# Index heads' columns first in the input projection, a split LayerNorm, and tile 1's transposes one weight piece later

## The reference

```
h = x @ w_in[i]
q, k, v, qi, ki, wi, u, vs = split(h)      # 512, 128, 128, 256, 64, 4, 512, 512 columns
rotate part of q, k, qi, ki
score = sum over 4 index heads of relu(qi . ki) * wi ; keep the 64 best keys of each row
a_out = attention over the kept keys
b_out = gelu(u) * (sgu_w (lower triangle) @ LayerNorm(gelu(vs)) + sgu_b)      # the gated half
x = LayerNorm(ALPHA * x + concat(a_out, b_out) @ w_o[i])
x = LayerNorm(ALPHA * x + (silu(gate) * up) @ w_ffn_out + (p[i] @ w_ple[i]) * sigmoid(x @ w_ple_gate[i]))
```

## Time and profile before

| | |
|---|---|
| median of three runs | 1430.33 us (1429.98 to 1430.45) |
| the profiled execution's own time | 1430.49 us |
| its span, first to last instruction | 1428.7 us |
| PE / DVE / ACT / POOL busy | 94% / 66% / 46% / 8% |
| dummy matmuls | 228 |

### The profile page before, as it was taken

The page is one execution under the profiler, slowest core; times in us unless marked ns, Lnnn a source line. Parts: engine busy times, 40 slices in busy tenths (PEclk is TensorE's granted clock), DMA queues, the critical chain, the costliest instruction groups (busy, mean ns, idle before and its releaser), DMA issues.

```text
span 1428.7 us, 16545 instructions
## 1 busy us (share of the span) xinstructions
PE 1342.2 (94%) x6684; PEld 1105.1 (77%) x6684; DVE 941.8 (66%) x1249; ACT 657.2 (46%) x886; POOL 109.8 (8%) x156
## 2 busy tenths in 40 slices
PE   6999999999989999999798898999998988999998
PEld 6767888887867788888598776888886866788886
DVE  4857677766675777775757857776766776554444
ACT  4544533333463543333365454454544554454542
POOL 1010000000020000000114300000002320000000
PEclk9999999999999999999998999999999998999999
DMA  9505577773712667776153213767673530355550
GB/s 363 199 1 206 209 308 293 295 279 126 272 60 77 227 245 294 292 295 220 61 183 104 90 56 120 293 240 290 238 292 114 181 118 1 118 206 188 188 184 30
DMA packets 40236, 269.87 MB, mean 189 GB/s; under 512 B 4544, under 2 KB 4560, under 8 KB 11872
## 3 DMA queue, kind: packets, MB, share of 16 engines
q1 hardware_dynamic: 37712, 259.31, 48.8%
q0 software_dynamic: 2304, 8.46, 1.6%
q10 hardware_dynamic: 144, 1.05, 0.2%
HBM read 267.75 MB, written 1.05 MB: 188 GB/s over the span
## 4 chain that ended last, share of the span: by engine, by line
PE 81%; DVE 11%; ACT 3%; issue 2%; POOL 1%; DMA 1%; SPq 0%; POOLq 0%; ACTq 0%; DVEq 0%
PE ps L1441 23%; PE ps L1443 23%; PE ps L1442 23%; PE ps L1466 4%; PE ps L1551 2%; DVE WB L1764 2%; PE ps L1527 1%; PE ps L1454 1%; PE ps L1426 1%; ACT WB L1564 1%; DMA RAW<-W 1%; DVE st L2027 1%; DVE X L2037 1%; DVE st L1957 1%; DVE X L2040 1%
## 5 line engine op out<-in xcount | busy, mean ns | idle before, releaser
L1764 DVE TENSOR_TENSOR WB<-RAW,WB 128x2048 fp32r<-128x2048 f32 (+4 forms) x210 | 453.2, 2161 | 267.4 <-ACT WB L1564 267.3
L1564 ACT ACTIVATE WB<-RAW 128x2048 fp32r<-128x2048 f32 (+4 forms) x210 | 379.7, 1810 | 232.8 <-PE ps L1443 219.6
L1441 PE MATMUL ps<-WB,XTH 128*128 128x512 f32 (+3 forms) x1176 | 457.9, 389 | 20.0 <-DVE XTL L1769 13.0
L1443 PE MATMUL ps<-WB,XTL 128*128 128x512 f32 (+3 forms) x1176 | 448.2, 381 | 0.0
L1442 PE MATMUL ps<-WB,XTH 128*128 128x512 f32 (+3 forms) x1176 | 447.5, 381 | 0.0
L1441 PEld LDWEIGHTS ps<-WB,XTH 128*128 128x128 f32 x1176 | 223.8, 190 | 60.6 <-DVE XTL L1769 13.3
L1443 PEld LDWEIGHTS ps<-WB,XTL 128*128 128x128 f32 x1176 | 222.9, 190 | 38.4
L1442 PEld LDWEIGHTS ps<-WB,XTH 128*128 128x128 f32 x1176 | 223.8, 190 | 34.9
L1441 PE MATMUL ps<-WB,HTH 128*128 128x512 f32 (+1 forms) x452 | 178.4, 395 | 2.5 <-DVE HTL L1845 2.0
L1443 PE MATMUL ps<-WB,HTL 128*128 128x512 f32 (+1 forms) x452 | 177.7, 393 | 0.0
L1442 PE MATMUL ps<-WB,HTH 128*128 128x512 f32 (+1 forms) x452 | 177.6, 393 | 0.0
(11 more groups left out here) (177 smaller groups left out, 1043.4 us busy)
## 6 DMA issues: line engine op xcount, KB each, us to landing
RAW<-W SPq DMA_DIRECT2D x220, 1024.0 KB, 4.9
RAW<-W SPq DMA_DIRECT2D x14, 768.0 KB, 4.3
RAW<-W SPq DMA_DIRECT2D x12, 728.0 KB, 6.0
VEC<-vecd POOLq DMA_DIRECT2D x10, 512.0 KB, 7.2
RAW<-W SPq DMA_DIRECT2D x8, 512.0 KB, 3.5
...
```

What stands on the lines that cost most here:

```text
L1441: eng.matmul(ps, xh, hi[:, j, c0:c0 + cw], start=first and j == 0, stop=False)
L1443: op = eng.matmul(ps, xl, hi[:, j, c0:c0 + cw], start=False, stop=last and j == n - 1)
L1564: return eng.activation(dst, src, f, **k)
L1764: eng.tensor_tensor(WB[:, it["raw"], 0:w], RAW[:, it["raw"], 0:w], WB[:, it["high"], 0:w].bitcast(F32), ALU.subtract).then_inc(*up("wl", n))
```

## The change

In layers 0 and 1 the columns of the index heads (324 of them) are the first chunk, vs the second, then q with k and v in two chunks of 384, then u. The rotation is two parts: `rope_sel` for the index heads early, `rope_qk` after the selection. Six transposes serve the index scores, twelve (q and k) come after the last chunk; DVE's rounds run beside the q, k, v chunks, and `sgu_ln` stands ahead of u. `p_split` stands between the fourth and the fifth round. Dummy matmuls change: four ahead of the sel_score are gone, the two fours ahead of transposes become twos, eight ahead of the attention's first transposes of E become two, and layer 1's eight ahead of its first scores become three. The first chunk of w_ple, now written to free columns of `H`, becomes filler of the attention. `ln_apply` is two parts, and its first pass no longer waits for the rsqrt; tile 1's LayerNorm of layers 0 and 1 has one `advance(1)` between the passes. `linear2` gets `mid_at=1` in w_ple_gate, even_w_in_2, odd_w_in_2 and both mlp_w1_2 (layer 1's w_in keeps 0). Tile 1's `gated_put` (in `last` its first half) stands ahead of `go(0)`, and the lows are pending during the last chunk of the even and odd output projections.

```diff
...
+
+        all_rows("w_in", i, 1024, (768, 1092), (1604, 2116), (0, 384), (384, 768), (1092, 1604))
+        all_rows("w_ple", i, 256, halves[0])
         all_rows("w_o", i, 1024, *halves)
-        all_rows("w_ple", i, 256, *halves)
+        all_rows("w_ple", i, 256, halves[1])
         all_rows("w_ple_gate", i, 1024, *halves)
         for c in range(12):
...
-        def ln_tile(key, t, after, between=None):
+
+        def ln_tile(key, t, after, between=None, before=None, halfway=None):
             sts, mv = col(12), col(2)
             do("ln_stats", key, t, sts, mv, after)
+            if before:
+                before()
             do("rsqrt", ("ln", key), mv[:, 1:2], 1.0, 1e-5, ("ln_mv", key))
             if between:
                 between()
-            do("ln_apply", key, t, mv)
+            do("ln_scale", key, t, mv)
+            if halfway:
+                halfway()
+            do("ln_shift", key, t, mv)
             return [("ln", key)]
...
-        def norm_tile(t, after):
+        def norm_sums(t, after):
             g = uid()
             ss = col(1)
             do("norm_sq", g, t, ss, after)
             do("rsqrt", ("nt", g), ss, 1.0 / D, 1e-6, ("norm_sq", g))
-            do("norm_apply", g, t, ss)
-            hn[t] = ("hn", g)
+
+            def apply():
+                do("norm_apply", g, t, ss)
+                hn[t] = ("hn", g)
+            return apply
+
+        def norm_tile(t, after):
+            norm_sums(t, after)()
 
...
+                    rope_sel(0)
+
             if i:
-                run(linear2("w_in", "x", xt_w, puts[0:2], mid_in, pad=(6, 0)))
+                fill = linear2("w_in", "x", xt_w, [put_sel, put_gelu(1)], mid_in, pad=(6, 0))
             else:
...
-                run(linear("w_in", "x", xt_w, puts[1]))
-            run(linear("w_in", "x", xt_w, puts[2]))
-            do("load_vec", i, 2, VEC[:, 2048:3072], vb + 4096, vec_free[2] + hw[0][0:1])
-            do("load_sg", i, t_pe)
+                run(linear("w_in", "x", xt_w, put_sel, touter=True))
+                fill = linear("w_in", "x", xt_w, put_gelu(1))
+            next(fill)
+            rope_sel(1)
...
+            do("load_vec", i, 2, VEC[:, 2048:3072], vb + 4096, vec_free[2])
             do("load_vec", i, 0, VEC[:, 0:1024], vb, vec_free[0])
             do("load_vec", i, 1, VEC[:, 1024:2048], vb + 1024, vec_free[1])
-            gw = [[], []]
-
-            def gelus():
-                for c in range(2):
-                    def put(t, b, done, c=c):
...
-                    yield from linear("w_in", "x", xt_w, put)
-
-            fill = gelus()
+            tws = []
             for t in range(2):
-                do("rope_in", i, t, hw[t] + mix_free[t], list(scr["free"]))
-                scr["free"] = [("kd", (i, t, 1))]
-            next(fill, None)
-            tw = []
-            for t in range(2):
-                src = ([H[:, t, j * 128:j * 128 + 128] for j in range(4)]
...
+            run(fill)
             for t in range(2):
                 do("sel_start", i, t)
                 for par in range(2):
                     b, fr = take()
-                    do("sel_score", i, t, par, b, tw, fr, e_free[par], 0 if t or par else 4)
+                    do("sel_score", i, t, par, b, tws, fr, e_free[par], 0)
                     give(b, ("sel_relu", (i, t, par)))
                     e_free[par] = [("sel_acc", (i, t, par))]
...
+            fill = chain(linear("w_in", "x", xt_w, put_in(1, 0, 384)), linear("w_in", "x", xt_w, put_in(2, 384, 768)))
             src = list(SCs)
             WK = [[SCR[:, 128:256], SCR[:, 0:128]], [SCR[:, 512:768], SCR[:, 256:512]]]
             for rnd in range(8):
+                if rnd % 2 == 0:
+                    next(fill, None)
+                if rnd == 4:
...
+                    do("p_split", i, list(pt_free))
                 mx8 = [col(8), col(8)]
                 dst = [WK[t][rnd % 2] for t in range(2)]
                 do("sel_round", i, rnd, mx8, src, dst)
                 src = dst
-                if rnd % 2:
-                    next(fill, None)
+            run(fill)
             do("sel_mask", i, src, list(sel_free))
             scr["free"] = [("sel", (i, t)) for t in range(2)]
-            run(fill)
-            do("sgu_ln", i, gw, [col(1) for _ in range(2)], [col(1) for _ in range(2)], [col(1) for _ in range(2)],
-               list(sq["free"]))
+            for t in range(2):
+                do("rope_qk", i, t, hw[t] + mix_free[t], list(scr["free"]))
+                scr["free"] = [("kd", (i, t, 1))]
+            do("sgu_ln", i, [list(gw[0]), list(gw[1])], [col(1) for _ in range(2)], [col(1) for _ in range(2)],
+               [col(1) for _ in range(2)], list(sq["free"]))
             sq["free"] = [("ln_ss", (i, 1))]
             vsw = [("sgu_ln", (i, t)) for t in range(2)]
             vec_free[2] = list(vsw)
-            do("p_split", i, list(pt_free))
+            run(linear("w_in", "x", xt_w, put_gelu(0)))
+            tw = []
+            for t in range(2):
+                tw += turn_T([H[:, t, j * 128:j * 128 + 128] for j in range(4)]
+                             + [MIX[:, t, j * 128:j * 128 + 128] for j in range(2)],
+                             [("kd", (i, t, 1))] + t_pe, 0, t, pad=0 if t else 2)
 
...
+                yield from linear("w_ple", "p", [[("pl", i)], [("pl", i)]], put_ple(0))
                 for gh in range(2):
                     b, fr = take()
                     do("gating", i, gh, b, vsw + fr)
                     give(b, ("gated", (i, gh)))
                     yield
             sgo = ("gated", (i, 1))
+
+            def put_ple(c):
+                def put(t, b, done):
+                    do("ple", (i, c, t), t, c, b, [done] + pt_free)
+                    give(b, ("ple", (i, c, t)))
+                return put
...
+                    if c and t:
+                        x_n[1] = ln_tile((i, 1, 1), 1, rw[1], halfway=lambda: advance(1))
                 return put
 
...
-            attention(units, 0.125, fill, pads=(8,), first=8 if i else 3)
+            attention(units, 0.125, fill, first=3)
...
             run(linear("w_o", "x", mo, put_o(1), touter=True,
                        mid=lambda: x_n.__setitem__(0, ln_tile((i, 1, 0), 0, rw[0]))))
-            x_n[1] = ln_tile((i, 1, 1), 1, rw[1])
...
-            for c in range(2):
-                def put(t, b, done, c=c):
-                    do("ple", (i, c, t), t, c, b, [done, sgo])
-                    give(b, ("ple", (i, c, t)))
-                run(linear("w_ple", "p", [[("pl", i)], [("pl", i)]], put))
+            run(linear("w_ple", "p", [[("pl", i)], [("pl", i)]], put_ple(1)))
...
+            run(linear2("w_ple_gate", "x", xt_w, [put_g(0), put_g(1)], mid1, pad=(0, 3), mid_at=1))
...
-                    elif t:
-                        norm_tile(0, x_n[0])
-                        go(0, pad=14)
-
-                x_n[t] = ln_tile((i, 2, t), t, [("add_out", (i, t, c)) for c in range(2)], between)
+
+                before = norm_sums(0, x_n[0]) if t and i else None
+                x_n[t] = ln_tile((i, 2, t), t, [("add_out", (i, t, c)) for c in range(2)], between, before,
+                                 (lambda: go(0, pad=14)) if t and i else None)
...
+                            pad=(10, 0), mid_at=1))
...
             def put(t, b, done):
+                gput(t, b, done)
                 if t:
                     go(0)
-                gput(t, b, done)
-                if t:
                     advance(1)
                     norm_tile(1, xg[1])
+
+            cur["lag"] = True
             run(linear(nm_out, "x", xo_w, put, touter=True, mid=lambda: norm_tile(0, xg[0])))
+            cur["lag"] = False
+            lows()
...
             def last(t, done):
-                if t and i == 0:
-                    go(0)
                 for c in range(2):
                     gated_put(i, c, 1, xg)(t, acc4[t][c][0], done[c])
+                    if t and c == 0 and i == 0:
+                        go(0)
                 if t:
                     advance(1)
...
-                act(GB[:, t, c * 512:c * 512 + 512], banks[b][:, :], ACT.Copy).then_inc(*up("ple", key))
+                act(PLE[:, t, c * 512:c * 512 + 512], banks[b][:, :], ACT.Copy).then_inc(*up("ple", key))
...
                 on.wait_ge(*at("gating", (i, gh)))
+                for t in range(2):
...
-            def ln_apply(key, t, mv):
+            def ln_scale(key, t, mv):
+                xs, n = X[:, t, :], 3 * (key[1] - 1)
+                on.wait_ge(*at("ln_mv", key))
+                on.wait_ge(*at("vec0", (key[0], n)))
+                eng.scalar_tensor_tensor(out=xs, in0=xs, scalar=mv[:, 0:1], in1=VEC[:, 0:1024], op0=ALU.subtract,
+                                         op1=ALU.mult).then_inc(*up("ln_scaled", key))
+
+            def ln_shift(key, t, mv):
                 xs, n = X[:, t, :], 3 * (key[1] - 1)
                 on.wait_ge(*at("rsqrt", ("ln", key)))
```

(5 more changed lines are left out.)

55 lines of the change are left out of this document (33 added, 22 removed).

## The result

The changed kernel takes 1415.93 us (median of 4 runs, 1413.07 to 1417.11) against 1430.15 (1429.73 to 1430.45) for the kernel before, run on the same chip: ratio 0.9898, 95% interval 0.9881 to 0.9915. It is 14.2 us faster where 27.3 were forecast, and lies 3 us above the forecast's range. The profiled execution had 1416.14 us, a span of 1414.3, so its distances can be set against the forecast's.

A forecast was written before the change was run, and what follows sets the result against it. PE was taken as the bound, busy 94% of the span at nearly full clock. Gains of 7.6 (layer 0), 8.8 (layer 1), 5.4, 2.4 and 3.3 sum to 27.5; 1430.49 less that is 1403.0 us, range 1394 to 1413.

The forecast's parts named there:

- The start: Start of the kernel, wider third weight piece: PE resumes tile 1 1.8 us late (0.5 to 2.5), clock 0.5 more.
- The projection: Layer 0 up to the first scores: gain 0.3 us (70.3 against 70.58), with 0.5 lost to POOL meeting rope_qk.
- The sum for DVE: Index scores to q and k transposes: DVE has 27.6 us of work, PE 29.4, so DVE fits by 1.8.
- the LayerNorm split: LayerNorm between statistics and first pass: DVE's 1.02 us wait for POOL becomes 0.8, a gain of 0.2.
- The clock: Half clock behind PE's idle time at the start: 0.5 us more, between 0 and 1.7.
- Rival B: PE runs at 1.2 GHz from the attention's start despite filler, with fewer dummies before it: 8.9 us, 1411.9; chance 0.11.
- Attention's start: First scores to the second gating's end: 13.9 us becomes 9.6, gain 4.3 in each of layers 0 and 1.
- The gate: End of w_o to the gate's tile 1: gain 3.0 us per layer, with a wait of 2.4 to 2.7.
- Layer 1's index rope: Layer 1: `rope_sel(1)` waits behind a low of the next piece, a hole of 1.1 us before the index transposes.
- Later stage changes: Gains of 5.4 us to the even block, 2.4 to the odd, 1.0 and 2.3 in even and odd feed-forward.
- New waits on `WB`: Sign of being right: new PE waits on DVE's `WB` of 1 to 2.5 us at each stage change.
- Rival D: All six stage changes: a1's low stands behind tile 1's norm, 32.6 us lost against 15.9 won, 1447; chance 0.03.

The follow-up runs named there:

- run 3: Changed kernel with the four POOL passes of `sgu_ln` (gain and bias) cut from 512 columns to 1: 1406.72 us.
- run 5: Changed kernel with `sgu_ln` whole put right behind the index scores, ahead of the q and k pieces: 1414.41 us.
- Run 6: Changed kernel with tile 1's index rope right behind tile 0's, ahead of the next piece's low on DVE: 1410.46 us.
- run 7: Changed kernel with only the gate's `mid_at` in the two layers back to 0: 1414.21 us.
- Run 8: Changed kernel with 14 dummy matmuls instead of 3 ahead of the first scores in both layers: 1412.51 us.
- run 9: Changed kernel with `sgu_ln` whole moved ahead of the third selection round: 1416.08 us.
- run 10: The kernel of run 9 with tile 1's index rope also put right behind tile 0's: 1413.64 us.
- run 13: Changed kernel, computation complete, with only POOL's four `sgu_ln` passes made to wait for the last q and k transposes: 1405.91 us.
- run 14: Changed kernel with the q and k rope ahead of the last two selection rounds, using `E` as scratch: 1415.08 us.
- run 15: Changed kernel with POOL's passes late, tile 1's index rope early, x's tile 1 split first, later index transposes and 9 gate dummies: 1397.18 us.
- run 1: The kernel before with the stage-change parts alone (`mid_at=1`, split LayerNorm, norm and gated-put order): 1418.93 us.

## Why the prediction was wrong, and where it was right

**The start**: tile 1's delay of 1.8 was right to 0.05, with some luck: other executions with the same start (runs 3, 5 to 10, 13 and 14) have tile 1 at 20.15 to 21.00. PE idled 3.99 there, 2.7 forecast. The clock's price was not right: 0.5 taken, 1.6 measured (tile 1's 24 products of 324 columns take 5.20, and 3.64 at full clock in run 3).

**The projection** is the first step that failed. It read: "`sgu_ln`'s four POOL operations (1.25 each) now meet rope_qk ... I take 0.5 lost (0 to 4)". DVE lost 4.1 in each layer, and the scores start 3.6 after PE's last transpose, where they start 0.9 after it in run 3; 1.6 were forecast. The row beside it, the p split of 1.60 for 0.6, said that a short operation pays a whole pass; each pass catches one, so four passes cost four times 1.0. The upper bound was the likely value: there was no ground for 0.5. The sum for DVE (27.6 against PE's 29.4, fits by 1.8) came out usable by luck. It took 5.3 for the score accumulation (4.1 in the trace) and 1.6 for the p split (0.7), and it left out two lows that stand between the rope and the copies of `T` (3.42). So the slack isn't 1.8: in run 3 the rope ends 3.0 before PE's last product, and behind the two lows DVE waits only 0.16 and 0.18 for PE's transposes. Of 4.1 us more on DVE, 3.1 arrive at the first scores in each layer (35.1 us from the index scores, 32.1 in run 3). With the passes out of the way the first scores start at 69.9 (runs 3 and 13, with x's tile 1 at 20.3; forecast 70.3 with it at 21.3), and PE waits 0.2. The Trainium skill (SBUF — State Buffer, Who interferes with whom) was cited for the LayerNorm split and not here, where the same rule, one blocking the other for a whole instruction, bears with four times the weight.

**The clock** is the second step that failed. The forecast priced it at 0.5, at the start alone. It expected waits of 2.4 to 2.7 in both gates and put no clock behind them, though its own row has the half clock behind a wait of 2.72. Rival B had the place for layer 0 (scores and w_ple take 6.5 at 74.0, and 3.7 in layer 1), but as a rival of 0.11, apart from the wait. It isn't apart: each hole of 2 us or more that the change opened was behind a late DVE operation, and four of six took the clock with them: 1.6 at 21.8, 2.8 at 74, 1.6 at 373, 1.6 at 472, in sum 7.6 where 0.5 was forecast. That is the profiled execution; the four executions of this kernel had 1413.07 us at a mean granted clock of 0.987, 1415.73 at 0.983, 1416.14 at 0.984 and 1417.11 at 0.982. Run 8 shows that filling the hole keeps the clock. That more dummies were needed as such is not shown: with no hole (runs 3, 13, 15) three are enough. The Trainium skill (TensorE: Matmul & The Clock Gate, What's actually happening) has full clock as what activity gives; the trace agrees, with the reservation below.

**Attention's start**: 4.3 forecast, 4.5 measured in layer 1 and 2.1 in layer 0, which is the half clock. First exp before PE asks, as said.

**The gate**: the wait on a1's low was forecast at 2.4 to 2.7 and measured 2.60 and 2.61; the gain 2.6 in layer 0 (3.0 forecast), 0.9 in layer 1 where the clock fell. That reordering the gate wins something by itself isn't shown by the times (runs 1 and 7).

**Layer 1's index rope**: a hole of 1.1 forecast, 0.36 and 2.10 measured. The mechanism was named; a low of 2.29 stands ahead of tile 0's rope and one of 1.75 ahead of tile 1's, and only one was counted. Run 6 returned it.

**Later stage changes**: 11.1 forecast, 12.0 measured, each within 0.6, run 1 confirms them alone. New waits on `WB` of 1.19 and 1.20 stand ahead of the even and the odd block; in the two feed-forward parts, where the forecast expected one too, PE has none of 1 us or more. The split of the LayerNorm gave 0.3 (PE's wait before the transposes after w_o fell from 0.60 to 0.30) for 0.2, and POOL's first operation took 1.21 beside the pass, for 0.19, as the forecast had it.

The misses in sum: the wait for `T` 2.0 over its forecast in each layer, the clock 7.1, the index rope 1.4, less 0.9 from the later stages: 11.6 of the 13.1 us between forecast and result. The other 1.5 I can't assign. Rival D's limit is a slip (15.9 won over six changes is 2.65 each, not 2.4), and nothing hangs on it. A wait was taken for a number by itself; its place in a chain of DVE work without a gap made it PE's wait for the most part (3.1 of 4.1 us), and PE's wait made it the clock's in layer 0.
